# Latent attention: scaled probabilities, values of two heads side by side, one running order of items

## The reference, cut to what matters

```python
q = rope(rms_norm(a_q @ w_uq) * q_gain)          # 512 x 16 x 96
k = rope(rms_norm([k_nope, k_pe]) * k_gain)      # 768 x 16 x 96
o = softmax(q @ k.T * 96 ** -0.5) @ v            # 512 x 16 x 64
x = x + gate * (o @ w_o)
```

## Time and profile before

| | us |
|---|---|
| median of 3 runs (3573.4 to 3576.97) | 3573.59 |
| the profiled execution | 3566.01 |
| its span on the core | 3564.2 |
| TensorE busy in it | 3321.1 (93%) |
| VectorE busy | 1509.7 (42%) |
| ScalarE busy | 1338.8 (38%) |
| GpSimd busy | 1316.8 (37%) |
| mean granted TensorE clock | 0.974 |

### The profile page before, as it was taken

How to read it: one execution, slowest core, us unless ns; L and a number is a source line. 1 busy time by engine, 2 the same in 40 slices (tenths; PEclk the granted TensorE clock), 3 DMA queues, 4 the chain that set the end, 5 groups by cost and what they waited for, 6 DMA issues and landing times.

```text
span 3564.2 us, 40787 instructions
## 1 busy us (share of the span) xinstructions
PE 3321.1 (93%) x16532; PEld 2654.3 (74%) x16532; DVE 1509.7 (42%) x2652; ACT 1338.8 (38%) x2304; POOL 1316.8 (37%) x730
## 2 busy tenths in 40 slices
PE   7989999999987889999989897899998989889998
PEld 4855788888845668788876687688887667768886
DVE  5557332222247774321224548342323555634142
ACT  4222331222245664432334524353333453434243
POOL 2224432222320001444561146644464025564446
PEclk9999999999989999999999999999999999999999
DMA  6134212112231000323232120323232112022322
GB/s 225 60 143 171 95 57 74 54 62 67 62 145 41 13 13 24 128 83 108 82 107 83 36 67 1 122 84 95 99 96 83 65 54 64 14 83 93 102 88 67
DMA packets 85639, 286.11 MB, mean 80 GB/s; under 512 B 9771, under 2 KB 10347, under 8 KB 84940
## 3 DMA queue, kind: packets, MB, share of 16 engines
q1 hardware_dynamic: 85452, 283.50, 24.1%
HBM read 281.37 MB, written 2.10 MB: 80 GB/s over the span
## 4 chain that ended last, share of the span: by engine, by line
PE 81%; DVE 11%; ACT 4%; DMA 2%; issue 1%; POOL 1%; SPq 0%; DVEq 0%; ACTq 0%
PE ps L443 20%; PE ps L446 20%; PE ps L444 20%; PE ps L468 2%; PE ps L469 2%; PE ps L470 2%; DMA ring<-in_w_mod 2%; PE ps L1874 1%; PE ps L1813 1%; DVE T L2423 1%; PE ps L492 1%; DVE sm L1819 1%; PE ps L1139 1%; PE ps L2095 1%; PE ps L1847 1%
## 5 line engine op out<-in xcount | busy, mean ns | idle before, releaser
L388 POOL TENSOR_TENSOR WL<-ring,WH 128x1024 fp32r<-128x1024 f32 (+2 forms) x443 | 958.5, 2167 | 1566.1 <-ACT WH L379 1565.5
L443 PE MATMUL ps<-HX,WH 128*128 128x512 f32 x1832 | 719.4, 393 | 4.6 <-POOL WL L388 4.6
L446 PE MATMUL ps<-HX,WL 128*128 128x512 f32 x1832 | 716.5, 391 | 0.0
L444 PE MATMUL ps<-HX,WH 128*128 128x512 f32 x1832 | 715.1, 390 | 0.0
L379 ACT CAST WH<-ring 128x1024 fp32r<-128x1024 f32 (+2 forms) x443 | 420.6, 951 | 427.1 <-PE ps L446 328.2
L443 PEld LDWEIGHTS ps<-HX,WH 128*128 128x128 f32 x1832 | 344.4, 188 | 84.6 <-POOL WL L388 5.9
L443 PE MATMUL ps<-FR,WH 128*128 128x512 f32 (+1 forms) x1072 | 400.2, 373 | 0.0
L444 PE MATMUL ps<-FR,WH 128*128 128x512 f32 (+1 forms) x1072 | 391.3, 372 | 0.0
L446 PEld LDWEIGHTS ps<-HX,WL 128*128 128x128 f32 x1832 | 345.6, 189 | 52.2
L444 PEld LDWEIGHTS ps<-HX,WH 128*128 128x128 f32 x1832 | 344.6, 188 | 51.4
L446 PE MATMUL ps<-FR,WL 128*128 128x512 f32 (+1 forms) x1072 | 371.0, 373 | 0.0
(11 more groups left out here) (335 smaller groups left out, 5310.0 us busy)
## 6 DMA issues: line engine op xcount, KB each, us to landing
ring<-in_w_mod SPq DMA_DIRECT2D x96, 512.0 KB, 5.4
ring<-in_ffn_w_up SPq DMA_DIRECT2D x88, 512.0 KB, 3.4
ring<-in_w_up SPq DMA_DIRECT2D x88, 512.0 KB, 3.5
ring<-in_w_in_tok SPq DMA_DIRECT2D x40, 512.0 KB, 3.5
ring<-in_w_in_feat SPq DMA_DIRECT2D x32, 512.0 KB, 3.4
ring<-in_ffn_w_down SPq DMA_DIRECT2D x32, 384.0 KB, 3.1
ring<-in_w_out SPq DMA_DIRECT2D x32, 384.0 KB, 3.1
ring<-in_w_down SPq DMA_DIRECT2D x32, 384.0 KB, 3.1
```

Of the source, the lines that this page charges most:

```text
L388: pool.tensor_tensor(WL[:, p % SPLITS, 0:n], ring.ap(r), WH[:, p % SPLITS, 0:n], ALU.subtract).then_inc(*ring.frees(r, split.g, "low", p))
L443: pe.matmul(o, high, xh, k == 0, False)
L444: pe.matmul(o, high, xl, False, False)
L446: m = pe.matmul(PS[bs[i]][:, 0:N], low, get(k)[0], False, k == g.kt - 1)
```

## The change

Items run through all four groups without a break: at step i of 69 item i is scored, item i-3 is transposed, and at i = 8q+11 the values of two heads over all 512 queries are multiplied, with V (64 columns) as the stationary operand, one head in partitions 0 to 63 of a bank and the other in 64 to 127. Two steps of the next group's heads are taken at each of items 5 to 14 of a group. The probabilities are divided by their sum on GpSimd, in P and ahead of the transposes; ScalarE copies all six transposed pieces, and every eighth item one result of 128x512. The query factor is no longer multiplied into the queries but given to the maximum and the exponential as a scale. The squares of the five batches are made by GpSimd. The output comes out with features in partitions, so that the transposes of O1 go; parts 0 to 5 are split at items 54 to 59, parts 6 and 7 from PSUM, and the projection's first two groups are interleaved (pair_pe). There are three P buffers, and PT holds two heads over all queries.

```diff
-        PT = buf(12480, 2, 768)
-        tabs = buf(14016, 4, 32)
-        QT = [buf(7360, 4, 512), buf(14144, 4, 512)]
-        KT = [buf(9408, 4, 768), buf(16192, 4, 768)]
+        PT = [T[:, 0:6, :], buf(12480, 6, 512)]
+        tabs = buf(15552, 4, 32)
+        QT = [buf(7360, 4, 512), buf(15680, 4, 512)]
+        KT = [buf(9408, 4, 768), buf(17728, 4, 768)]
         VT = [buf(5824, 6, 256), CX[:, :, :].rearrange("p a b -> p (a b)")[:, 0:1536].rearrange("p (a b) -> p a b", a=6)]
-        O1 = buf(20480, 4, 1024)
-        Pb = buf(24576, 2, 768)
-        scr = buf(26112, 768)
+        OT = buf(20800, 8, 512)
+        Pb = [buf(24896, 768), buf(25664, 768), T[:, 6:8, :].rearrange("p a b -> p (a b)")[:, 0:768]]
+        scr = buf(26432, 768)
+        scr_rope = CX[:, :, :].rearrange("p a b -> p (a b)")[:, 1536:1792]
+        rq, nrq = (sm[:, x:x + 32].rearrange("p (g i) -> p g i", g=2) for x in (0, 32))
         st = sm[:, 224:256]
...
         def heads_pe(pe, n):
...
+                if t % 2:
+                    yield
...
-            for _ in range(12):
+                if t % 2:
+                    yield
...
         def heads_a(act, n):
...
+            for step in range(4, STEPS - 4):
+                x = (step - 4) // 2
+                if step % 2 == 0 and x < 5:
+                    act.wait_ge(*mla.v.at("mean", n, x))
+                    act.activation(st2[:, 0:8], st2[:, 0:8], ACT.Sqrt, scale=96.0 if x < 2 else 1.0).then_inc(
+                        *mla.a.up("root", n, x))
...
+        def heads_g(pool, n):
+            for step in range(STEPS):
+                x = (step - 3) // 2
+                if step % 2 and 0 <= x < 5:
+                    pool.wait_ge(*(mla.a.at("q", n, 2 * x + 1) if x < 2 else mla.a.at("kv", n, 2 * x - 3)))
+                    if x >= 2:
+                        pool.wait_ge(*mla.v.at("kpe", n))
+                    if (n, x) != (0, 0):
+                        pool.wait_ge(*mla.v.at("mean", *((n, x - 1) if x else (n - 1, 4))))
+                    pool.tensor_tensor(scr3, batch(x), batch(x), ALU.mult).then_inc(*mla.g.up("square", n, x))
+                yield
+
...
+            for step in range(STEPS - 4):
+                x = (step - 4) // 2
+                if step == 4:
+                    dve.wait_ge(*mla.v.at("kpe"))
+                    if n:
+                        dve.wait_ge(*mla.pe.at("turn", n - 1, 3, 2))
+                    for t in range(6):
+                        dve.tensor_copy(ktok[:, t, :].rearrange("p (h c) -> p h c", h=4)[:, :, 64:96],
+                                        kpe[:, t, :].unsqueeze(1).to_broadcast([128, 4, 32])).then_inc(*mla.v.up())
+                    mla.v.mark("kpe", n)
+                if step % 2 == 0 and 0 <= x < 5:
+                    mean_v(dve, n, x)
+                elif step % 2 and 0 <= x < 5:
+                    factor_v(dve, n, x)
+                if step == 8:
+                    dve.wait_ge(*lds["rope"])
+                    rope_v(dve, qtok.rearrange("p t (h c) -> p t h c", h=4))
+                elif step == 14:
+                    rope_v(dve, ktok[:, 0:4, :].rearrange("p t (h c) -> p t h c", h=4))
+                    mla.v.mark("heads", n)
                 yield
...
+        def mean_v(dve, n, x):
+            dve.wait_ge(*mla.g.at("square", n, x))
+            dve.wait_ge(*mla.v.now())
+            dve.tensor_reduce(st2[:, 0:8], scr3, AX, ALU.add).then_inc(*mla.v.up())
+            dve.wait_ge(*mla.v.now())
+            if x < 2:
+                by_tile = st2[:, 0:8].rearrange("p (t h) -> p t h", h=4)
+                e = epsq[:, 2 * x:2 * x + 2].unsqueeze(2).to_broadcast([128, 2, 4])
+                dve.scalar_tensor_tensor(by_tile, by_tile, 1.0 / 96, e, ALU.mult, ALU.add).then_inc(*mla.v.up("mean", n, x))
+            else:
+                dve.tensor_scalar(st2[:, 0:8], st2[:, 0:8], 1.0 / 96, EPS, ALU.mult, ALU.add).then_inc(
+                    *mla.v.up("mean", n, x))
+        def factor_v(dve, n, x):
+            x3, g = batch(x), n % 2
+            dve.wait_ge(*mla.a.at("root", n, x))
+            if x < 2:
+                if n >= 2:
+                    dve.wait_ge(*att.a.at("exp", 16 * n - 17, 1))
+                    dve.wait_ge(*att.v.at("max", 16 * n - 17))
+                c = slice(8 * x, 8 * x + 8)
+                dve.reciprocal(rq[:, g, c], st2[:, 0:8]).then_inc(*mla.v.up())
+                dve.wait_ge(*mla.v.now())
+                dve.tensor_scalar(nrq[:, g, c], rq[:, g, c], -1.0, None, ALU.mult).then_inc(*mla.v.up())
+                dve.tensor_tensor(x3, x3, rows[:, 0:96].unsqueeze(1).to_broadcast([128, 8, 96]), ALU.mult).then_inc(
+                    *mla.v.up())
+                return
+            dve.reciprocal(st2[:, 0:8], st2[:, 0:8]).then_inc(*mla.v.up())
+            dve.wait_ge(*mla.v.now())
+            dve.tensor_tensor(x3, x3, st2[:, 0:8].unsqueeze(2).to_broadcast([128, 8, 96]), ALU.mult).then_inc(*mla.v.up())
+            dve.wait_ge(*mla.v.now())
+            dve.tensor_tensor(x3[:, :, 64:96], x3[:, :, 64:96], rows[:, 160:192].unsqueeze(1).to_broadcast([128, 8, 32]),
+                              ALU.mult).then_inc(*mla.v.up())
...
+        CUTS = ((0, 512), (512, 768))
+        def lat_scores_pe(pe, i):
+            n, h, t = item(i)
+            for j, (c0, c1) in enumerate(CUTS):
+                b = bank.take("ls", i, j)
+                pe.wait_ge(*bank.free("ls", i, j))
+                pe.wait_ge(*mla.v.at("made", n))
+                pe.wait_ge(*mla.a.at("made", n))
+                pe.matmul(PS[b][:, 0:c1 - c0], QT[n % 2][0:96, h, t * 128:t * 128 + 128], KT[n % 2][0:96, h, c0:c1], True,
+                          True).then_inc(*att.pe.up("scores", i, j))
+        def lat_max_v(dve, i):
+            s8 = sums(i)
+            if i >= 4:
+                dve.wait_ge(*att.g.at("scaled", i - 4))
+                dve.wait_ge(*att.a.at("exp", i - 4, 1))
+            for j, (c0, c1) in enumerate(CUTS):
+                dve.wait_ge(*att.pe.at("scores", i, j))
+                dve.tensor_reduce(s8[:, j:j + 1], ps("ls", i, j)[:, 0:c1 - c0], AX, ALU.max).then_inc(*att.v.up())
+            dve.wait_ge(*att.v.now())
+            dve.scalar_tensor_tensor(s8[:, 2:3], s8[:, 0:1], s8[:, 1:2], factor(nrq, i), ALU.max, ALU.mult).then_inc(
+                *att.v.up("max", i))
+        def lat_exp_a(act, i):
+            s8 = sums(i)
+            act.wait_ge(*att.v.at("max", i))
+            if i >= 3:
+                act.wait_ge(*att.pe.at("turn", i - 3, 1))
+            for j, (c0, c1) in enumerate(CUTS):
+                act.activation(Pb[i % 3][:, c0:c1], ps("ls", i, j)[:, 0:c1 - c0], ACT.Exp, bias=s8[:, 2:3],
+                               scale=factor(rq, i), accum_out=s8[:, 3 + j:4 + j]).then_inc(
+                    *bank.emptied(("ls", i, j), att.a, "exp", i, j))
+        def lat_sum_v(dve, i):
+            s8 = sums(i)
+            dve.wait_ge(*att.a.at("exp", i, 1))
+            dve.tensor_tensor(s8[:, 5:6], s8[:, 3:4], s8[:, 4:5], ALU.add).then_inc(*att.v.up())
+            dve.wait_ge(*att.v.now())
+            dve.reciprocal(s8[:, 5:6], s8[:, 5:6]).then_inc(*att.v.up("sum", i))
+        def lat_scale_g(pool, i):
+            pool.wait_ge(*att.v.at("sum", i))
+            pool.wait_ge(*att.a.at("exp", i, 1))
+            pool.tensor_tensor(Pb[i % 3], Pb[i % 3], sums(i)[:, 5:6].to_broadcast([128, 768]), ALU.mult).then_inc(
+                *att.g.up("scaled", i))
+        def lat_turn_pe(pe, i):
+            for x in range(2):
+                b = bank.take("lt", i, x)
+                pe.wait_ge(*bank.free("lt", i, x))
+                pe.wait_ge(*att.g.at("scaled", i))
+                for j in range(4 * x, 4 + 2 * x):
+                    m = pe.transpose(PS[b][:, (j - 4 * x) * 128:(j - 4 * x) * 128 + 128],
+                                     Pb[i % 3][:, j * 128:j * 128 + 128], ident[:, :])
+                m.then_inc(*att.pe.up("turn", i, x))
+        def lat_turn_a(act, i):
+            n, h, t = item(i)
+            if i >= 8:
+                act.wait_ge(*att.pe.at("values", i // 8 - 1))
+            for x in range(2):
+                act.wait_ge(*att.pe.at("turn", i, x))
+                k = 4 - 2 * x
+                act.copy(PT[h % 2][:, 4 * x:4 * x + k, t * 128:t * 128 + 128],
+                         ps("lt", i, x)[:, 0:128 * k].rearrange("p (a b) -> p a b", a=k)).then_inc(
+                    *bank.emptied(("lt", i, x), att.a, "turned", i, x))
+        def lat_values_pe(pe, q):
+            n, two = divmod(q, 2)
+            b = bank.take("lv", q)
+            pe.wait_ge(*bank.free("lv", q))
+            pe.wait_ge(*att.a.at("turned", 8 * q + 7, 1))
+            for j in range(6):
+                for x in range(2):
+                    c = (2 * two + x) * 64
+                    m = pe.matmul(PS[b][64 * x:64 * x + 64, :], VT[n % 2][:, j, c:c + 64], PT[x][:, j, :], j == 0, j == 5)
+            m.then_inc(*att.pe.up("values", q))
```

(71 more changed lines are left out.)

163 lines of the change are left out of this document (47 added, 116 removed).

## The result

The changed kernel takes 3606.14 us (median of 4 runs, 3601.95 to 3610.26), the kernel before 3574.36 (4 runs, 3573.4 to 3576.97): a ratio of 1.0088, 95% interval 1.007 to 1.0105. It is slower by 0.9%, inside the range and 9 us under the predicted time. Between the two profiled executions the span grew by 43.0 us (3564.2 to 3607.2), between the medians by 31.8; a profiled execution is a single one of its kernel, and the one of the kernel before was 8 us faster than its median.

What follows compares the result with a forecast made beforehand. TensorE was taken to bound latent attention, its saving outweighed by a chain through GpSimd and VectorE: stage +32.2, prologue +3, clock +6, +41 us on the 3573.6 median, 3615 us, range 3597 to 3634.

Steps and rivals of the forecast that it cites:

- The chain: Items 7 to 11: scaling, square, reduction, root follow in series, 8.2 us a query batch, 8.4 a key batch, 44.6 a group.
- the burst is hidden: Item 11: the values' burst on TensorE adds no time because it runs within the chain.
- the root at 0.28 us: ScalarE's root in each batch of the chain, counted at 0.28 us.
- Items 5 and 6: Each group: q projection 5.15 us and four of six kv 3.45 on TensorE; maximum 7 done at 11.3 us.
- The pace of the light items: Items without heads' steps: scaling 0.09 + 1.85, then maximum and sum 0.48, so 2.4 us each.
- A burst: Values of eight items on TensorE: 24 records in 5.15 us, plus a hand-over loss, 5.4 us.
- The hold: VectorE's maximum of SBUF operands waits until GpSimd's scaling beside it is done, whatever the size; part of 2.4 us an item.
- Clock: TensorE drops partly to 1.2 GHz in the chains, slowing the heads' transposes: +2 us a group, +6 in all.
- M(5): Time when item 5's maximum is done, taken as group start; first at 14.4 us into the stage.
- Rival (a): Squares are ready when VectorE comes; chain items take 4.4 us, total -16 us, 3558 us; chance 0.11.
- Rival (b): No hold for single columns and a scaling of 0.92 us: total +18 us, 3592 us; chance 0.19.
- Rival (c): Column tiles of the values run in turn, five unhidden bursts, 26 us more: total +67, 3641 us; chance 0.06.

Runs made afterwards that it cites:

- Run 1: Changed kernel with GpSimd scaling item i-1 instead of item i, ahead of the heads' steps, so squares run before the scaling: 3598.9 us, ratio 1.0063.
- run 9: Changed kernel with nothing on GpSimd: VectorE scales the probabilities with tensor_scalar and makes the squares: 3599.0 us, ratio 1.0071.
- run 3: Changed kernel with the transposes of item i-3 put ahead of the values on TensorE: 3594.15 us, ratio 1.005.
- run 4: Changed kernel with VectorE's subtraction of a converted output part taken one item later, behind the next maxima: 3600.3 us, ratio 1.0059.
- run 6: Run 1 with the heads' steps spread over the group by a table instead of two at each of items 5 to 14: 3587.32 us, ratio 1.0041.
- run 12: run 11 with the squares made by ScalarE (ACT.Square) instead of VectorE: 3551.08 us, ratio 0.9937.
- run 8: run 7 with one root for two or three batches, two pairs of table loads a group instead of five, head steps moved to suit: 3575.89 us, ratio 1.0012.
- run 7: Changed kernel with the edits of Run 1, run 3, run 4 and run 6 together: 3572.27 us, ratio 0.9996.
- run 11: run 7 with scaling and squares on VectorE, nothing on GpSimd, and one root for two or three batches: 3566.39 us, ratio 0.9981.

## Why the prediction was right, and where its steps were off

The sign held, and the loss lies in the one stage: TensorE's saving was given back to a chain of hand-overs in items 7 to 11. The mechanism held in part. The chain is there as it was described, but the link that the prediction blamed, GpSimd's scaling and square, came last by only about 1 us an item. Run 1 took it out and got 6.9 us back, run 9 left GpSimd out altogether and got 6.4. The bursts (12.4 us, run 3), the output parts at the end (9.1, run 4) and the crowding of the heads' steps into ten items (10.0, run 6) each cost more. So a good part of the agreement of the total is luck. The profile shows +42.8 us in the stage where 32.2 + 6 were forecast, and +0.3 in the prologue for +3, where single executions scatter by 10: +43.0 in the span for +41. By its terms:

- **The chain** (44.6 us a group forecast, rope included): the maxima of items 7 and 12 are 44.69 us apart. The agreement is errors that cancel. GpSimd's operation took 1.47 us, not 1.85, two of them in each of five items, 3.8 us less; the burst at item 11, said to be hidden in the chain, was 4.4 us longer than the step before it. **That the burst is hidden is the step that failed.** It reckoned only with the values' own inputs, not with the transposes that stand behind the burst on TensorE and the buffer that ScalarE's exponentials want from them; run 3 shows it, with 13.4 us at four such places. The second step that failed is the root at 0.28 us: each root has a function table load of 1.28 us ahead of it and one behind it, and on ScalarE stands behind exponentials and copies. That path is nearly as long as the one over GpSimd, and the sum had nothing for it.
- **Items 5 and 6** of a group (11.3): 12.5.
- **The pace of the light items** (2.4 forecast): 1.95 us. The loop by the prediction's own formula, with 1.47 for 1.85, is 0.09 + 1.47 + 0.48 = 2.04; items 2 to 4 show that loop at 1.83, and behind them TensorE's 1.95 is what shows. The mis-sized term is the scaling again. The row chosen for it was an operation of the same shape on three different tensors with a rounded output; here one operand is the output's own buffer and the other a broadcast factor or the same tensor. The lower end taken for it was 0.92 and the upper 2.15. By the prediction's own sign (wrong if items 0 to 4 run at 2.0) this term is wrong.
- **A burst** (5.4): in the light part the 24 records take 5.3 us at the full clock, as said (0.43 a pair). The step at item 3 of a group is 9.17 against 1.95, 7.2 more: behind the burst stand a transposition, then scores, then a maximum before the next item can go on. 1.8 us too small, three times, and at item 59 11.6 instead of 7.8.
- **The hold** of VectorE by GpSimd is real, for one column too, but was placed wrongly. 59 of the 64 maxima escaped it, in the light items by 0.1 us; copies and rope products did not (six copies 3.45 us for 0.89; a product 1.59 for 0.28, as below), which the sum did not have:

```profile
1209.45 3.45 DVE L1797 COPY AR<-AR 128x128 f32<-128x128 f32 x6
1209.62 1.50 POOL L1908 TENSOR_TENSOR AR<-AR,sm 128x768 f32<-128x768 f32 x1 [3.92 <-DVE sm L1903]
```

- **Items 54 to 58** (4.5 each): 5.24, then 4.63 four times.
- **Items 12 to 16** (15.2 us for the key rope, a group's four heads' transposes and three items): 17.6. The transposes of the first heads ran at the lower level: 20 of them took 4.18 us, the next 20 2.39.
- **Clock** (+6): 0.76 in the chain, 0.83 over the stage. TensorE's work was to fall by 41 us and its busy time fell by 15.5 (266.3 to 250.8); in run 12, with a clock of 0.93, it is 237.3. A matmul at the lower level counts as busy for longer (1.06 us for 0.59 in the burst of item 11), so these sums mix work and clock. What the clock costs on the path was not measured by itself; the 0.85 us pitch of item 11's values and the 4.18 us of transposes are 2.7 + 1.8 us a group, more than the 2 forecast.
- **Start of the stage:** M(5) came 11.3 us behind the first scores, not 14.4: the first item takes 1.29 us and the next four 1.82 to 2.11, not 2.4.
- **VectorE's wait** for the 15 squares was to be about 4 us each; it was 36.3 us in all, 2.4 each.
- **The median:** the prediction added the 7.6 us by which the profiled execution before was under its median; the one after was 3 us above its own. That is why a sum that was 2 us under the profile is 9 over the median.

Rival (a), squares that don't wait, was put at -16 us. Run 1 made just that and got 334.0, 36 us above the kernel before: rival (a) was wrong in its own terms, because what is left of the chain is 6.2 to 9.0 us an item, not 4.4. Rival (b) needed a scaling at 0.92 us and no hold for single columns; the scaling took 1.47, and a single column was held (0.61 for 0.22). Rival (c), column tiles in turn, is out: two tiles ran side by side, a pair every 0.43 us.

That two column tiles double the rate agrees with the Trainium skill ("TensorEngine Tiling (Array Packing)", Performance Considerations). The drain at a change of tiling mode, which the same page names under Key Properties, does not stand out at the burst's start: the second pair begins 0.45 us behind the first, the others 0.43. The Trainium skill ("SBUF — State Buffer", SBUF: two separate sides) says that VectorE with two SBUF inputs and GpSimd exclude each other for a whole instruction. The kernel after and run 8 agree, down to 128x1 (0.61 and 0.67 for 0.22 us). Copies and a negation with one SBUF tensor are held too (3.45 for 0.89, 1.44 for 0.17); the same section says that VectorE in a two-port mode excludes GpSimd as well, and whether these ran in it no row here tells.

What stays open is how much of the stage the clock costs, in the kernel after and in run 12, and what the new form of the values is worth alone: no run has it in the old order, or the old form in the new order. That VectorE's own work sets the pace before run 12 is shown for four of the five items that had a square in groups 1 and 2 (items 4, 5, 9 and 10): each got 1.0 us shorter when its square of 0.95 us went to ScalarE. The fifth, item 11 with the burst, got 0.4 and 1.9 us shorter, and the clock of the stage went from 0.90 to 0.93. So that the stage lost 13.6 us for 14.3 us of squares is in part chance.

## What to carry to other kernels

Work taken off a busy engine is worth what the slowest ring of hand-overs leaves of it: write down, for one item, which engine's next instruction waits for which, and put every new instruction into that ring before counting it. A batch of work saved up for one moment (here values of eight items) blocks everything queued behind it; place it behind the small instructions that other engines want first. Before using GpSimd as a free engine, check what VectorE does at the same time from SBUF: here VectorE did the same scaling in 0.62 us where GpSimd took 1.47. A long wait in the profile is worth only as much as it outlasts the next path: here 3.00 us of waiting for GpSimd hid 0.96 us of cost. The one version that beats the kernel before by more than 0.2% (run 12, 0.6%) puts together all the moves of runs 1, 3, 4 and 6, fewer roots, the scaling on VectorE and the squares on ScalarE; the last step alone brought 15 us, and what it would bring without the others was not run.

## What the runs showed of the hardware

- A product of 128x768 on GpSimd takes 1.47 us when both inputs are one tensor or one is a broadcast column, against 1.85 for three different tensors with a rounded output; which of the two differences counts no run tells apart. The hold goes both ways: beside a VectorE product that was itself held, the square took 2.2 us (run 7):

```profile
1216.09 2.22 DVE L1845 TENSOR_TENSOR AR<-AR,sm 128x768 f32<-128x768 f32 x1
1217.45 2.18 POOL L1786 TENSOR_TENSOR AR<-AR 128x768 f32<-128x768 f32 x1
```

- VectorE's tensor_scalar on 128x768 fp32 in SBUF takes 0.62 us, a tensor_tensor of the same shape 0.95 to 0.96.
- ScalarE's exponential of 128x512 takes 0.78 us with a factor column as its scale, 0.69 before with a number (bias from a column in both).
- A function table load is 1.28 us, and ScalarE's Square needed none between exponentials (13 loads in the stage in run 11 and in run 12).
